# A weight ring of five laid elsewhere in SBUF, and its first loads moved in the DMA queue

## What is computed

```python
mod = silu(c) @ ada_w + ada_b;  sh1, sc1, g1, sh2, sc2, g2 = split(mod, 6)
h = rms_norm(x) * (1 + sc1) + sh1
x = x + g1 * hybrid_mixer(h)       # 8 heads of banded, 8 of forgetting attention,
                                   # merged by gates: m = sig(ga)*ua + sig(gb)*ub; m @ w_out
h = rms_norm(x) * (1 + sc2) + sh2
# mixture of experts: 64 experts of 256 hidden units, 8 per token, plus a shared one
idx, w = top8_of_4_groups(sigmoid(h @ w_router) + bias)
routed = sum_e w_e * (silu(h @ Wg_e) * (h @ Wu_e)) @ Wd_e
shared = (silu(h @ Wg_s) * (h @ Wu_s)) @ Wd_s
out = x + g2 * (routed + shared)
```

## Time and profile before

| | |
|---|---|
| median of 3 runs | 1336.86 us (1336.18 to 1339.76) |
| the profiled execution | 1335.73 us, its span 1333.9 us |
| PE busy | 1229.2 us, 92% of the span |
| DVE, ACT, POOL busy | 469.5, 198.4, 195.3 us |
| chain that ended last | PE 68%, DMA 22%, DVE 4% |
| moved by DMA | 311.50 MB, 234 GB/s on the mean |
| mean granted PE clock | 0.968 of 2.4 GHz |

### The profile page before, as it was taken

The page is one execution under the profiler, slowest core; times in us unless marked ns, Lnnn a source line. Parts: engine busy times, 40 slices in busy tenths (PEclk is TensorE's granted clock), DMA queues, the critical chain, the costliest instruction groups (busy, mean ns, idle before and its releaser), DMA issues.

```text
span 1333.9 us, 14005 instructions
## 1 busy us (share of the span) xinstructions
PE 1229.2 (92%) x4703; PEld 625.1 (47%) x4703; DVE 469.5 (35%) x1252; ACT 198.4 (15%) x449; POOL 195.3 (15%) x219
## 2 busy tenths in 40 slices
PE   5999999999999999997999999898898989898993
PEld 4564454444688644444444444344343334344442
DVE  3653580500366322455333333223222323232232
ACT  4010000110465201120011011000010001010100
POOL 0000000000222000000022322221121221122222
PEclk9989999999999999998999999899898989899996
DMA  9964651221100302161499989999999998999962
GB/s 305 367 207 144 219 177 63 98 91 63 63 1 0 127 0 103 63 252 68 150 392 377 319 315 382 399 383 373 369 365 381 344 368 328 378 365 366 371 172 32
DMA packets 88301, 311.50 MB, mean 234 GB/s; under 512 B 13200, under 2 KB 38960, under 8 KB 63024
## 3 DMA queue, kind: packets, MB, share of 16 engines
q1 hardware_dynamic: 70992, 272.77, 52.7%
q0 software_dynamic: 15808, 35.69, 10.8%
q10 hardware_dynamic: 1440, 2.27, 0.5%
HBM read 297.56 MB, written 36.18 MB: 250 GB/s over the span
## 4 chain that ended last, share of the span: by engine, by line
PE 68%; DMA 22%; DVE 4%; SPq 2%; issue 2%; ACT 0%; POOL 0%; POOLq 0%; DVEq 0%; ACTq 0%
PE PS L1313 19%; PE PS L1591 17%; DMA R_XM<-w_up_e 11%; PE PS L1612 8%; DMA R_WT<-w_up_e 6%; PE PS L1471 4%; PE PS L1442 4%; PE PS L1375 2%; PE PS L1577 2%; PE PS L1351 2%; PE PS L1481 2%; DVE R_A L865 1%; PE PS L1363 1%; DMA R_WT<-ada_w 1%; DMA out<-second_sum 1%
## 5 line engine op out<-in xcount | busy, mean ns | idle before, releaser
L1313 PE MATMUL PS<-R_WT,R_HT 128*128 128x512 f32 x640 | 277.8, 596 | 1.1 <-DVE R_HT L889 1.1
L1591 PE MATMUL PS<-R_WT,R_G 128*64 128x512 f32 (+1 forms) x432 | 170.0, 643 | 31.5 <-DMA R_XM<-w_up_e 22.2
L1313 PEld LDWEIGHTS PS<-R_WT,R_HT 128*128 128x128 f32 x640 | 122.4, 192 | 153.5 <-issue 152.2
L1591 PE MATMUL PS<-R_Z,R_G 128*128 128x512 f32 (+1 forms) x464 | 169.0, 624 | 16.5 <-DMA R_Z<-w_up_e 16.5
L1179 DVE TENSOR_TENSOR R_G<-R_G,PS 128x256 f32<-128x256 f32 x50 | 30.4, 609 | 391.0 <-ACT R_G L812 391.0
L1591 PEld LDWEIGHTS PS<-R_WT,R_G 128*64 128x64 f32 (+1 forms) x432 | 60.5, 168 | 131.9 <-issue 131.9
L1591 PEld LDWEIGHTS PS<-R_Z,R_G 128*128 128x128 f32 (+1 forms) x464 | 65.6, 170 | 111.9 <-issue 111.9
L611 POOL DMA_INDIRECT out<-R_G,ridx x37 | 55.8, 1508 | 359.9 <-DVE R_G L1200 238.4
L817 ACT ACTIVATE R_G<-PS 128x256 f32<-128x256 f32 x50 | 19.2, 384 | 590.7 <-PE PS L1599 575.1
L1591 PE MATMUL PS<-R_XM,R_G 128*64 128x512 f32 (+1 forms) x208 | 102.2, 648 | 0.0
L1200 DVE SCALAR_TENSOR_TENSOR R_G<-PS,slx,R_XM 128x512 f32<-128x512 f32 x100 | 75.1, 751 | 67.3 <-PE PS L1612 67.3
(11 more groups left out here) (235 smaller groups left out, 1227.0 us busy)
## 6 DMA issues: line engine op xcount, KB each, us to landing
R_Z<-w_gate_e SPq DMA_DIRECT2D x26, 1024.0 KB, 13.8
R_Z<-w_up_e SPq DMA_DIRECT2D x26, 1024.0 KB, 23.7
R_Z<-w_down_e SPq DMA_DIRECT2D x26, 1024.0 KB, 19.0
R_WT<-w_gate_e SPq DMA_DIRECT2D x26, 1024.0 KB, 13.8
R_WT<-w_up_e SPq DMA_DIRECT2D x26, 1024.0 KB, 24.1
R_WT<-w_down_e SPq DMA_DIRECT2D x26, 1024.0 KB, 17.8
R_WT<-w_in SPq DMA_DIRECT2D x10, 2048.0 KB, 8.3
R_WT<-ada_w SPq DMA_DIRECT2D x18, 1024.0 KB, 10.9
```

What stands on the lines that cost most here:

```text
L1313: ins = mm(PS[:, t, :], HT[:, k, P * t:P * t + P], WR[:, b, k, :], start=k == 0, stop=k == KD - 1)
L1591: ins = mm(PS[w * h:w * h + w, b, :].rearrange("p (g n) -> p g n", g=2), XT[:, b, k, w * h:w * h + w], WGU[n][:, k], start=k == 0, stop=k ...
```

## The change

The five places of the ring lie elsewhere. Expert 0's lies over the merge weights, expert 1's over the projections and w_out, the third over x and two modulation rows, the fourth and fifth partly over the shared weights and over h2 transposed. Gate/up and down of a place need no longer be neighbours. The shared and router weights go to other places as well, and DVE reuses one quarter of G's second half in the output projection, so that w_down_s can lie in the rest. Shared rows are written to three row buffers (SHR) instead of over x, in the order 1, 0, 2, 3; row 3 reuses the buffer of row 1 and waits until that is stored; ScalarE stores the rows in this order, each with a semaphore of its own.

SP's order becomes: w_out; router, shared gate and up right behind it; after the merge (s_u) expert 0; after s_m the shared down; h2 rows 0 and 1 with their x rows; after the output projection (s_o) expert 1; rows 2 and 3; then the tables. The third load waits for x to be stored (s_out), the fourth and fifth for the shared gate and up and the router, and none of the three waits for the shared down or for the stored sum.

```diff
--- before.py
+++ after.py
@@ -210,9 +210,10 @@
         WO = R_Z[:, 0:8192].rearrange("p (k n) -> p k n", k=KD)
         H2T = YT
 
-        WSGU = R_W[:, 0:4096].rearrange("p (g k n) -> p k g n", g=2, k=KD)
-        WSD = R_W[:, 4096:6144].rearrange("p (k n) -> p k n", k=2)
-        WRT = R_W[:, 6144:6656].rearrange("p (k n) -> p k n", k=KD)
+        WSGU = R_Z[:, 8192:12288].rearrange("p (g k n) -> p k g n", g=2, k=KD)
+        WSD = R_G[:, 5632:7680].rearrange("p (k n) -> p k n", k=2)
+        WRT = R_WT[:, 12288:12800].rearrange("p (k n) -> p k n", k=KD)
+        SHR = [R_HT[:, 1856:2880], R_HT[:, 2880:3904], R_A[:, :]]
         SILS = R_S[:, 1024:2048].rearrange("p (t n) -> p t n", t=NT)
         ACTS = R_S[:, 2048:3072].rearrange("p (t n) -> p t n", t=NT)
 
@@ -228,9 +229,10 @@
         SCT = R_A[0:E, 0:512]
         Q1T, WTT = R_A[0:E, 0:512], R_A[0:E, 512:1024]
 
-        WX = [r[:, 6144 * n:6144 * (n + 1)] for r in (R_Z, R_WT) for n in range(2)] + [R_XM[:, 0:6144]]
-        WGU = [w[:, 0:4096].rearrange("p (g k n) -> p k g n", g=2, k=KD) for w in WX]
-        WDN = [w[:, 4096:6144].rearrange("p (k n) -> p k n", k=2) for w in WX]
+        GU_AT = [R_WT[:, 0:4096], R_Z[:, 0:4096], R_XM[:, 0:4096], R_Z[:, 8192:12288], R_WT[:, 8192:12288]]
+        DOWN_AT = [R_WT[:, 4096:6144], R_Z[:, 4096:6144], R_XM[:, 4096:6144], R_Z[:, 6144:8192], R_WT[:, 6144:8192]]
+        WGU = [w.rearrange("p (g k n) -> p k g n", g=2, k=KD) for w in GU_AT]
+        WDN = [w.rearrange("p (k n) -> p k n", k=2) for w in DOWN_AT]
         XG = R_G[:, 0:2048].rearrange("p (b n) -> p b n", b=2)
         XT = R_G[:, 2048:4096].rearrange("p (b k s) -> p b k s", b=2, k=KD)
         SIL = R_G[:, 4096:4608].rearrange("p (b n) -> p b n", b=2)
@@ -323,7 +325,8 @@
             "onehot_ready", "slots_done", "slot_rows_ready", "x_transposed", "xt_ready_dve",
             "xt_ready_act", "gu_done", "silu_ready", "act_ready", "act_transposed", "at_ready",
             "down_done", "o_ready", "row_index_ready"))
-        s_out, s_sout = sem("residual_written"), sem("shared_written")
+        s_out = sem("residual_written")
+        s_sout = [sem(f"shared_written{t}") for t in range(NT)]
         s_idle = sem("idle")
         s_dch, s_ach, s_pch = map(sem, ("dve_chain", "act_chain", "pool_chain"))
 
@@ -483,51 +486,53 @@
             sp.dma_start(WPB, a["w_proj_b"].rearrange("(k p) n -> p k n", p=P)).then_inc(s_wp, 16)
             sp.wait_ge(s_yt, 8)
             sp.dma_start(WO, a["w_out"].rearrange("(k p) n -> p k n", p=P)).then_inc(s_wo, 16)
-            sp.wait_ge(s_u, 8)
-            sp.dma_start(R_W[:, 6144:6656], a["w_router"].rearrange("(p k) n -> p (k n)", p=P)).then_inc(s_ws, 16)
-            sp.dma_start(R_W[:, 0:2048], a["w_gate_s"].rearrange("(p k) n -> p (k n)", p=P)).then_inc(s_ws, 16)
-            sp.dma_start(R_W[:, 2048:4096], a["w_up_s"].rearrange("(p k) n -> p (k n)", p=P)).then_inc(s_ws, 16)
-            sp.dma_start(R_W[:, 4096:6144], a["w_down_s"].rearrange("(p k) n -> p (k n)", p=P)).then_inc(s_ws, 16)
-            for t in range(NT):
+            sp.dma_start(R_WT[:, 12288:12800], a["w_router"].rearrange("(p k) n -> p (k n)", p=P)).then_inc(s_ws, 16)
+            sp.dma_start(R_Z[:, 8192:10240], a["w_gate_s"].rearrange("(p k) n -> p (k n)", p=P)).then_inc(s_ws, 16)
+            sp.dma_start(R_Z[:, 10240:12288], a["w_up_s"].rearrange("(p k) n -> p (k n)", p=P)).then_inc(s_ws, 16)
+
+            def load_gate_up(n, e):
+                sp.dma_start(GU_AT[n][:, 0:2048], a["w_gate_e"][bass.ds(e, 1)].rearrange(
+                    "o (p k) n -> p (o k n)", p=P)).then_inc(s_wgu[n], 16)
+                sp.dma_start(GU_AT[n][:, 2048:4096], a["w_up_e"][bass.ds(e, 1)].rearrange(
+                    "o (p k) n -> p (o k n)", p=P)).then_inc(s_wgu[n], 16)
+
+            def load_down(n, e):
+                sp.dma_start(DOWN_AT[n], a["w_down_e"][bass.ds(e, 1)].rearrange(
+                    "o (p k) n -> p (o k n)", p=P)).then_inc(s_wd[n], 16)
+
+            def expert(c):
+                return sp.value_load(etab[0:1, bass.ds(c, 1)], min_val=0, max_val=E - 1)
+
+            def write_rows(t):
                 sp.wait_ge(s_h2, t + 1)
                 sp.dma_start(h2_dram[P * t:P * (t + 1), :], HROW[:, t % 2]).then_inc(s_hb[t % 2], 16)
                 sp.dma_start(a["out"][P * t:P * (t + 1), :], X[:, t, :]).then_inc(s_out, 16)
 
-            def load_gate_up(n, e):
-                sp.dma_start(WX[n][:, 0:2048], a["w_gate_e"][bass.ds(e, 1)].rearrange(
-                    "o (p k) n -> p (o k n)", p=P)).then_inc(s_wgu[n], 16)
-                sp.dma_start(WX[n][:, 2048:4096], a["w_up_e"][bass.ds(e, 1)].rearrange(
-                    "o (p k) n -> p (o k n)", p=P)).then_inc(s_wgu[n], 16)
-
-            def load_down(n, e):
-                sp.dma_start(WX[n][:, 4096:6144], a["w_down_e"][bass.ds(e, 1)].rearrange(
-                    "o (p k) n -> p (o k n)", p=P)).then_inc(s_wd[n], 16)
-
-            def expert(c):
-                return sp.value_load(etab[0:1, bass.ds(c, 1)], min_val=0, max_val=E - 1)
-
+            sp.wait_ge(s_u, 8)
+            load_gate_up(0, 0)
+            load_down(0, 0)
+            sp.wait_ge(s_m, 8)
+            sp.dma_start(R_G[:, 5632:7680], a["w_down_s"].rearrange("(p k) n -> p (k n)", p=P)).then_inc(s_ws, 16)
+            write_rows(0)
+            write_rows(1)
             sp.wait_ge(s_o, 8)
-            for q in range(2):
-                load_gate_up(q, q)
-                load_down(q, q)
+            load_gate_up(1, 1)
+            load_down(1, 1)
+            write_rows(2)
+            write_rows(3)
             sp.wait_ge(s_tabs, 1)
             nblk = sp.value_load(nover[0:1, 0:1], min_val=0, max_val=NEXT - 4) + NM
             for q in range(2, E):
                 n, e = q % NRING, expert(LOADS[q])
-                if q == NRING - 1:
-                    sp.wait_ge(s_h2, NT)
-                    sp.wait_ge(s_sout, 16 * NT)
+                if q == 2:
+                    sp.wait_ge(s_out, 16 * NT)
                 elif q < NRING:
                     sp.wait_ge(s_sgu, NT)
                     sp.wait_ge(s_rt, 1)
                 else:
                     sp.wait_ge(s_gu, LAST[q - NRING] + 1)
                 load_gate_up(n, e)
-                if q < NRING - 1:
-                    sp.wait_ge(s_sdn, 2 * NT)
-                elif q == NRING - 1:
-                    pass
-                else:
+                if q >= NRING:
                     sp.wait_ge(s_dn, 2 * (LAST[q - NRING] + 1))
                 load_down(n, e)
 
@@ -638,7 +643,8 @@
                 gather(j, j % 2)
             nblk = pool.value_load(nover[0:1, 0:1], min_val=0, max_val=NEXT - 4) + NM
             pool.wait_ge(s_out, 16 * NT)
-            pool.wait_ge(s_sout, 16 * NT)
+            for t in range(NT):
+                pool.wait_ge(s_sout[t], 16)
             for j in range(NM):
                 if j == NM - TAIL:
                     join_sums()
@@ -823,9 +829,9 @@
             take_xt(1, 1)
             silu(0, 0)
             shared_at(3)
-            for t in range(NT):
-                act.wait_ge(s_sx, max(4, 2 * t + 2))
-                act.dma_start(sum_dram[P * t:P * (t + 1), :], X[:, t, :]).then_inc(s_sout, 16)
+            for n, t in enumerate((1, 0, 2, 3)):
+                act.wait_ge(s_sx, 2 * n + 2)
+                act.dma_start(sum_dram[P * t:P * (t + 1), :], SHR[n % 3]).then_inc(s_sout[t], 16)
             act.wait_ge(s_tabs, 1)
             nblk = act.value_load(nover[0:1, 0:1], min_val=0, max_val=NEXT - 4) + NM
 
@@ -1025,8 +1031,8 @@
             for n in range(8):
                 t, cols = n // 2, slice(512 * (n % 2), 512 * (n % 2) + 512)
                 dve.wait_ge(s_o, n + 1)
-                link(dve.tensor_tensor(G[:, 1, t, cols], PS[:, n % 4, :], MOD[:, 2, cols], ALU.mult))
-                dve.tensor_tensor(X[:, t, cols], X[:, t, cols], G[:, 1, t, cols], ALU.add).then_inc(s_x2, 1)
+                link(dve.tensor_tensor(G[:, 1, 0, cols], PS[:, n % 4, :], MOD[:, 2, cols], ALU.mult))
+                dve.tensor_tensor(X[:, t, cols], X[:, t, cols], G[:, 1, 0, cols], ALU.add).then_inc(s_x2, 1)
                 if n % 2 and t:
                     h2_rows(t - 1)
             h2_rows(NT - 1)
@@ -1122,10 +1128,13 @@
 
             def shared_rows(t):
 
+                row = SHR[(1, 0, 2, 3).index(t) % 3]
+                if t == 3:
+                    dve.wait_ge(s_sout[1], 16)
                 for n in range(2 * t, 2 * t + 2):
                     cols = slice(512 * (n % 2), 512 * (n % 2) + 512)
                     dve.wait_ge(s_sdn, n + 1)
-                    dve.tensor_tensor(X[:, t, cols], PS[:, (0 if t == 1 else 2) + n % 2, :], MOD[:, 3, cols], ALU.mult)\
+                    dve.tensor_tensor(row[:, cols], PS[:, (0 if t == 1 else 2) + n % 2, :], MOD[:, 3, cols], ALU.mult)\
                         .then_inc(s_sx, 1)
 
 
@@ -1210,7 +1219,6 @@
             onehot(1, 1)
             slots(0, 0)
```

(1 more changed line is left out.)

## The result

The changed kernel takes 1344.09 us (median of 4 runs, 1341.78 to 1345.96) against 1337.03 of the kernel before. The ratio is 1.0043, with a 95% interval of 1.0025 to 1.0060: it is slower, by some 5.7 us. (The medians of these few runs are 7.1 us apart.) Of all the executions in this document two, at 2134.52 us (kernel before) and 1445.58 us (run held for gather 0 alone), fell in a slower state of the chip and are left out of every ratio. The median lies 1.1 us above the prediction's range, which ends at 1343.0; the ratio, put on the 1336.86 us from which the prediction started, gives 1342.6, just inside it. Either way it is rival B's end of the range: the likeliest case had + 1.7. The span of the profiled execution grew from 1333.9 to 1340.0 us.

The account below looks back on a forecast made before the run. A chain of small steps was taken to bound the kernel up to 637.68 us, PE to 820, then weight loads. The gathers' + 1.7 us and 0 for all else gave 1338.6 us, range 1335.5 to 1343.0.

Parts of the forecast that it names:

- rival B: First two gathers at the slow end and PE's clock falls as well: + 5.1 us, say 1342.0 us; chance 23%.
- the likeliest case: Whole kernel: slower gathers delay PE's start by 1.7 us, everything else 0; 1338.6 us, chance 50%.
- The lead of the loads is worth nothing in the third regime: Stretch after 820 us, where weight loads end last: earlier loads gain 0 while PE has no wait before 796.
- The shared weights, experts 0 and 1, the row writes, G, the shared rows: 0: Before PE's first expert matmul at 637.68: moved loads, row writes, reused buffer and shared rows each cost 0.
- The first two gathers: Before the first expert matmul: second gather lands 2.3 us later beside queued loads, 0.6 in hand: + 1.7 us.
- The sentence on equal halves: DMA queues at the gathers: equal halves would give some 200 GB/s and no delay; the measured split speaks against it.
- The clock: PE around the gathers' transposes: granted clock stays full, cost 0; if it falls, 1.8 us, or 3.6.
- The signs: Trace marks: nine expert issues 626 to 632, second gather after 636.5, first expert matmul 638 to 642, stalls 47 to 49.
- The new wait of DVE: DVE's shared row 3 waits for row 1's write, taken to land in 8.7 us, hidden by 3.7 us: 0.
- Rivals A: Expert weight loads: their lead survives and removes stalls, at most all 48.0 us (1289 us); chance 8%.
- C: DVE's wait for row 1's write binds: 5.0 us on top of 1.7, 1343.6 us; chance 3%.
- D: First two gathers lose nothing because their rows pass the loads fast enough: 1336.9 us; chance 16%.

Follow-up runs that it names:

- run held for gather 0 alone: Changed kernel with all nine transfers of the third to fifth load held until the first block's gather has landed: ratio 0.9985 to the kernel before.
- run with all nine held to the shared down: Changed kernel with all nine transfers of the third to fifth load held until the shared down matmuls are done: ratio 1.0043 to the kernel before.
- run with seven held: Changed kernel, third load's gate and up issued at the tables, the other seven expert transfers held until the first two gathers landed: ratio 1.0001 to the kernel before.
- short rows: Changed kernel with the nine transfers of the third to fifth load each cut in two, with 4 KB DRAM rows: ratio 1.0038 to the kernel before.
- run with six fillers: Changed kernel with six extra matmuls, products unused, in PE's waits for the first two gathers: ratio 1.0037 to the kernel before.
- five issued: Changed kernel with five of nine expert transfers issued at the tables, four held until the first two gathers landed: ratio 1.0055 to the kernel before.

## Why the prediction was right or wrong

- **The lead of the loads is worth nothing in the third regime: right.** The stalls for up weights behind 820 are 44.5 to 49.7 us in all twelve kernels, with the early loads, without them, or held. The gap ahead of SP's issue is there after as before. The step had set a condition, no wait of PE before 796; what it did not work out is when this breaks, which the run with all nine held to the shared down found (5.0 us).
- **The shared weights, experts 0 and 1, the row writes, G, the shared rows: 0, right** to within the interval, by the run with seven held (1.0001). The row writes behind expert 1 landed in 4.2 to 5.8 us instead of 2.6 and nobody waited.
- **The first two gathers: the mechanism right, the size wrong.** This is the term that failed: + 1.7 us, where the delay ahead of PE's second transposes measured 4.55. Two steps of it were off. "Until 633.6 nothing differs" was wrong: by then the gathers had moved 0.03 MB since 631 and not 0.14, because the load queue was running out before and is full now. So 0.43 MB were left and not 0.32. And the rate was 61 GB/s (0.43 MB from 633.6 to 640.6, 0.5 us before the landing) where I took 75. With both put right the same sum closes: 7.0 us instead of 2, less the 0.6 in hand, + 4.4. The slower row alone, 54, would have given + 3.3, still short.
- **What was there to be read.** 116 was the largest of four ends of later gathers in the kernel before; the others moved 0.18 MB in 3.7 us, 0.29 in 4.1 and 0.23 in 3.8, which is 49, 71 and 61 GB/s. Better still is the whole landing of a gather. In the kernel before, the gathers at 671.3 and 680.3 met a full load queue and a scatter, and took 11.9 and 12.4 us to land. Those at 647.2 and 657.6 met few loads or none and landed in 4.4 and 4.2 us. The first two, with 6.2 and 6.0, were the case in between.
- **The sentence on equal halves** stands: the page's rule (the Trainium skill, "DMA: Bandwidth & Descriptors", "Queues, rings and completion order") speaks of turns by packet, and equal halves were not seen: 0.47 MB against 3.81. The run with short rows (9.1 instead of 11.2 us) shows that the length of a load's rows matters. It does not test the rule itself: a packet on that page is a group of descriptors, often 9 to 17, and no run shows whether the profile's packets, at most 8 KB here, are the same thing.
- **The clock: wrong in the likeliest case, right as half of rival B.** I left it at full; it was at 0.50 from 637.25 to 642. The waits of 1.70 and 0.83 us before had left it at full, and so did 1.04 and 0.95 in the run with six fillers; with 3.05 and 1.80 (changed kernel), 3.73 and 1.46 (short rows) and 4.34 and 2.08 (five issued) it fell. The price, 1.8 by the row of the shared down, was 1.40 by the sum and 1.3 by the fillers.
- **Rival B, + 5.1 us, 23%**, is what happened: 4.55 + 1.40 = 5.95 in the trace, 5.7 by the ratio. That its sum of 5.1 came so close is partly luck: its wait was too small (3.3) and its price of the clock too large (1.8). It had half the chance of the forecast, yet its two parts hang together: the longer the gather, the longer PE idles, and in all three runs with the long waits the clock fell. The prediction gave 0.68 to a change within 4.0 us; some 5.7 is outside.
- **The signs.** The nine issues, the late landing of gather 1, the DMA share that dips in the same place and the half clock in block 0 came as foretold. PE's first expert matmul stands at 642.84, 0.8 us behind the 638 to 642 that were named, and the stalls are 49.4 us where 47 to 49 were named.
- **The new wait of DVE: 0, right.** The write was issued at 650.67 and landed 8.3 us later; DVE came to it at 663.13, 4.2 us after that (3.7 predicted). Rivals A, C and D did not happen.

## What to carry to other kernels

A transfer that is moved earlier does not only arrive earlier; it also stands in the queue beside whatever moves then. Before you release bulk loads, find the small transfer on the critical path in that stretch and let it land first: one wait for two gathers turned the changed kernel from 0.43% slower into 0.18% faster, and made the kernel before 0.27% faster. And where a ring is released by the consumer and the queue runs empty once, a head start ahead of that gap was worth nothing here, as long as the first load was in time.

## What the runs showed of the hardware

- Small gathers beside a full load queue got 47 GB/s of 423, and the harm was the same with 5 MB queued as with 9: the second lands in 10.9 and 11.2 us. With 2 MB both land in 5.7 to 6.2 us, with none in 4.3 to 5.1.
- An issue on SP can take far longer than 0.33 us; why, no run was made to show. Examples are 2.11 and 4.25 us with twelve and thirteen others issued since 659.25, in the run with the loads held to the shared down.
- The granted clock can fall within a wait of 3.05 us: it was 1.00 from 634 up to 637.0 in the changed kernel and 0.50 from 637.25, with PE idle since 634.26.
